# LayerNorm's sums over partitions: an fp32 matmul replaced by two in the linear products' format

## The reference

```python
def _layer_norm(x, g, b):
    mu = mean(x); var = mean(square(x - mu))          # over the channels
    return (x - mu) * rsqrt(var + 1e-5) * g + b

proj = x @ w_in                                       # 1024 -> 1792
attn = window_attention(q, k, v)                      # chunks of 64, window 128, sinks
c    = silu(_layer_norm(dwconv31(u1 * sigmoid(u2)), conv_ln_g, conv_ln_b))   # 512 channels
h    = _layer_norm(ALPHA * x + concat(attn, c) @ w_out, ln1_g, ln1_b)        # 1024
upc  = dwconv3(h @ w_up)                              # 1024 -> 5632
f    = (silu(upc[:D_FF]) * upc[D_FF:]) @ w_down       # 2816 -> 1024
y    = _layer_norm(ALPHA * h + f + sigmoid(h @ w_pg + b_pg) * (p @ w_pe), ln2_g, ln2_b)
```

## Time and profile before

| | |
|---|---|
| median of three runs | 2401.93 us |
| the profiled execution | 2402.03 us, span 2400.1 us |
| TensorE matmuls | 2356.6 us busy, 12733 instructions |
| VectorE | 1388.5 us busy, 2021 instructions |
| ScalarE | 1149.9 us busy |
| GpSimd | 1358.5 us busy, of it 1345.6 in L543 |
| TensorE's mean granted clock | 0.996 of full speed |

### The profile page before, as it was taken

The page is one execution under the profiler, slowest core; times in us unless marked ns, Lnnn a source line. Parts: engine busy times, 40 slices in busy tenths (PEclk is TensorE's granted clock), DMA queues, the critical chain, the costliest instruction groups (busy, mean ns, idle before and its releaser), DMA issues.

```text
span 2400.1 us, 32895 instructions
## 1 busy us (share of the span) xinstructions
PE 2356.6 (98%) x12733; PEld 2189.2 (91%) x12733; DVE 1388.5 (58%) x2021; ACT 1149.9 (48%) x1873; POOL 1358.5 (57%) x1078
## 2 busy tenths in 40 slices
PE   7999999999999999999999999999999999999997
PEld 7988999999988899899998999899889999999996
DVE  5946777634666666426766665257666652663232
ACT  3545654443565443425553535236635353574452
POOL 6654566565644555457545454676555546666663
PEclk9999999999999999999999999999999999999999
DMA  5432334344433333353432332444333324354432
GB/s 190 122 118 88 122 113 126 117 132 145 123 126 111 97 106 107 96 171 108 136 112 89 107 120 82 148 144 146 106 97 106 115 87 153 118 164 139 140 119 86
DMA packets 99978, 289.77 MB, mean 121 GB/s; under 512 B 13424, under 2 KB 37104, under 8 KB 99824
## 3 DMA queue, kind: packets, MB, share of 16 engines
q1 hardware_dynamic: 82560, 261.77, 35.2%
q10 hardware_dynamic: 17264, 25.91, 3.3%
HBM read 278.74 MB, written 8.99 MB: 120 GB/s over the span
## 4 chain that ended last, share of the span: by engine, by line
PE 94%; ACT 2%; DVE 2%; POOL 1%; issue 1%; DMA 0%; DVEq 0%; SPq 0%; ACTq 0%
PE ps L611 30%; PE ps L612 30%; PE ps L613 30%; POOL w_lo L543 1%; PE ps L670 1%; PE ps L702 1%; PE ps L690 1%; PE ps L679 1%; PE ps L717 0%; DVE sq L1329 0%; ACT w_hi L789 0%; DMA x_raw<-in_xT 0%; DMA a_raw<-in_xT 0%; PE ps L751 0%; PE ps L742 0%
## 5 line engine op out<-in xcount | busy, mean ns | idle before, releaser
L543 POOL TENSOR_TENSOR w_lo<-w_raw,w_hi 128x512 fp32r<-128x512 f32 (+2 forms) x1060 | 1345.6, 1296 | 1004.0 <-ACT w_hi L789 998.4
L789 ACT CAST w_hi<-w_raw 128x1024 fp32r<-128x1024 f32 (+2 forms) x529 | 517.0, 982 | 565.0 <-PE ps L613 493.9
L611 PE MATMUL ps<-h_hi,w_hi 128*128 128x450 f32 (+5 forms) x2080 | 743.1, 357 | 7.7 <-POOL w_lo L543 7.7
L612 PE MATMUL ps<-h_lo,w_hi 128*128 128x450 f32 (+5 forms) x2080 | 736.1, 354 | 0.0
L613 PE MATMUL ps<-h_hi,w_lo 128*128 128x450 f32 (+5 forms) x2080 | 735.3, 353 | 0.0
L611 PEld LDWEIGHTS ps<-h_hi,w_hi 128*128 128x128 f32 x2080 | 392.7, 189 | 38.9 <-POOL w_lo L543 9.6
L612 PEld LDWEIGHTS ps<-h_lo,w_hi 128*128 128x128 f32 x2080 | 392.7, 189 | 22.1 <-issue 1.5
L613 PEld LDWEIGHTS ps<-h_hi,w_lo 128*128 128x128 f32 x2080 | 392.3, 189 | 21.1
L611 PE MATMUL ps<-f_hi,w_hi 128*128 128x448 f32 (+2 forms) x1072 | 383.1, 357 | 0.0
L612 PE MATMUL ps<-f_lo,w_hi 128*128 128x448 f32 (+2 forms) x1072 | 377.4, 352 | 0.0
L613 PE MATMUL ps<-f_hi,w_lo 128*128 128x448 f32 (+2 forms) x1072 | 377.4, 352 | 0.0
(11 more groups left out here) (155 smaller groups left out, 1923.1 us busy)
## 6 DMA issues: line engine op xcount, KB each, us to landing
w_raw<-in_panels SPq DMA_DIRECT2D x450, 512.0 KB, 3.5
w_raw<-in_panels SPq DMA_DIRECT2D x40, 384.0 KB, 3.0
xres<-in_xT ACTq DMA_DIRECT2D x24, 224.0 KB, 2.8
out_yT<-res ACTq DMA_DIRECT2D x3, 1792.0 KB, 6.4
w_raw<-in_panels SPq DMA_DIRECT2D x40, 128.0 KB, 2.1
a_raw<-in_xT ACTq DMA_DIRECT2D x4, 896.0 KB, 5.9
x_raw<-in_xT SPq DMA_DIRECT2D x2, 896.0 KB, 5.6
a_raw<-in_xT ACTq DMA_DIRECT2D x2, 768.0 KB, 6.3
```

Of the source, the lines that this page charges most:

```text
L543: ins = pool.tensor_tensor(w_lo[:, n % WS, c], w_raw[:, n % RS, c], w_hi[:, n % WS, c].bitcast(F32), ALU.subtract)
L611: pe.matmul(out, w_hi[:, sl, c], hi, start=first, stop=False)
L612: pe.matmul(out, w_hi[:, sl, c], lo, start=False, stop=False)
L789: act.copy(w_hi[:, n % WS, 0:w], w_raw[:, n % RS, 0:w]).then_inc(w_hi_done, 1)
```

## The change

Twelve of the fifteen LayerNorms are touched, for the mean and the variance each. After the last add, VectorE multiplies the block by 1 (for `cln` by 2) with an output in fp32r, which gives the high part `sum_hi`, and computes the low part `sum_lo` as block times 1 or 2 minus `sum_hi`. TensorE multiplies both by a tile `ones8` of 1/1024 in fp32r and adds them up in PSUM, in place of one f32 matmul. `ones8` is made once by ScalarE from `mean8`. The last add of `tree` and of `running_sum` no longer reports to TensorE but is waited for on VectorE itself.

```diff
+    sum_hi = place("sum_hi", [WM], F32R, offset=sq_base + HB * WM * 4)
+    sum_lo = place("sum_lo", [WM], F32R, offset=sq_base + (HB + 1) * WM * 4)
...
+    ones8 = place("ones8", [P], F32R)
...
                 pe.wait_ge(arrived, SUM_NO[name, t] + 1)
-                pe.matmul(ps[:, b, 0:WIDTH[t]], ones[:], sq[:, 0, 0:WIDTH[t]], start=True, stop=True).then_inc(done, 1)
+                pe.matmul(ps[:, b, 0:WIDTH[t]], ones8[:], sum_hi[:, 0:WIDTH[t]], start=True, stop=False)
+                pe.matmul(ps[:, b, 0:WIDTH[t]], ones8[:], sum_lo[:, 0:WIDTH[t]], start=False, stop=True).then_inc(done, 1)
...
                         act.wait_ge(zero_set, 1)
+                        act.copy(ones8[:], mean8[:])
...
             def tree(src, nb, w, done):
+                blocks = nb
                 while nb > 1:
                     nb //= 2
                     ins = dve.tensor_tensor(sq[:, 0:nb, 0:w], src[:, 0:nb, :], src[:, nb:2 * nb, :], ALU.add)
                     src = sq[:, :, 0:w]
-                    if nb > 1:
-                        own.step(ins)
-                        own.wait()
-                ins.then_inc(done, 1)
+                    own.step(ins)
+                    own.wait()
+                split_sum(w, done, blocks)
+
+            def split_sum(w, done, blocks):
+
+                times, total = float(KB // blocks), sq[:, 0, 0:w]
+                own.step(dve.tensor_scalar(sum_hi[:, 0:w], total, times, None, ALU.mult))
+                own.wait()
+                dve.scalar_tensor_tensor(sum_lo[:, 0:w], total, times, sum_hi[:, 0:w].bitcast(F32), ALU.mult, ALU.subtract
+                                         ).then_inc(done, 1)
...
                 ins = dve.tensor_tensor(total, h_raw[:, 0, c] if m == 1 else total, h_raw[:, m, c], ALU.add)
+                own.step(ins)
                 if m == KB - 1:
-                    ins.then_inc(sum_done, 1)
-                else:
-                    own.step(ins)
+                    own.wait()
+                    split_sum(w, sum_done, KB)
```

## The result

The changed kernel takes 2414.84 us (median of five, 2413.03 to 2415.26) against 2402.0 us: a ratio of 1.005, 95% interval 1.0039 to 1.0061. It is slower by 12.8 us, in the direction to which 0.42 of the chances went, but outside the range of 2399 to 2411. The profiled execution took 2415.03 us, span 2413.1.

What follows compares the result with a forecast made beforehand. TensorE, busy 98% of the span, was taken to bound the kernel. Hold-ups of 12.0 us less a gain of 7.9 made +4.1 us on the profiled 2402.03 (median 2401.93): forecast 2406.0 us, range 2399 to 2411.

Steps and rivals of the forecast that it cites:

- TensorE's gain, 7.9 us: At 24 mean and variance matmuls, fp32r pairs replace f32 products: 0.345 us saved at 448 columns, less at narrower, 7.9 total.
- worth this in full: On TensorE's queue: the whole 7.9 us saved shortens the kernel, since TensorE sets the end.
- The price of the two instructions and the double wait for GpSimd: On VectorE after each sum: about 1.1 us alone, 3.05 us when both instructions wait for GpSimd's halves.
- Rival A: At VectorE's split: tensor_scalar does not contend with GpSimd, hold-ups are half as long, net -2.3, 2399.6 us; chance 0.13.
- Where it reaches TensorE: Ahead of mean matmuls: nine places where TensorE comes too soon after the sum, 0.2 to 3.0 us each, 12.0 together.
- rival C: Behind waits at 1651 and 2058 us: TensorE's granted clock falls, about 1.7 us each, +7.5, 2409.4 us; chance 0.12.
- I add nothing: VectorE work queued behind the split: delays cost 0, covered by several groups of about 4 us through five PSUM banks.
- one of my signs of being wrong: Ahead of L611, TensorE's linear products: a wait that was not there before would show the forecast wrong.
- Range and chances: Whole kernel: 2399 to 2411 us; faster 0.08, no change 0.50, slower 0.42.

Runs made afterwards that it cites:

- TensorE's part alone: Changed kernel without VectorE's split: the last add writes the sum into sum_hi in fp32r, TensorE multiplies it twice, no low part; 2398.39 us, 0.9983 of the original kernel.
- The third run: Changed kernel with the whole sum put in PSUM instead of SBUF, nothing else changed; 2403.86 us, 1.0008 of the original kernel.
- kept-busy: Changed kernel with 16, 18 and 9 overwritten filling matmuls on TensorE in the three longest waits; 2410.25 us, 1.0032 of the original kernel.
- step run: TensorE's part alone plus one f32 product of 8 columns behind each fp32r pair, 24 in all; 2400.49 us, 0.9990 of the original kernel.

## Why the prediction was wrong

- **TensorE's gain, 7.9 us: right in kind, too large.** The spacing at one mean was read rightly (0.36 saved, 0.345 forecast). The term assumed that nothing else on TensorE changes; by the table 7.0 us came in, and 5.65 in the trace of TensorE's part alone. The linear products behind some means now step 4 ns longer, and "worth this in full" leaves out that a TensorE that comes earlier waits longer for `w_lo` at three places (0.6 us) and gains next to nothing where it waits for the sum.
- **The price of the two instructions and the double wait for GpSimd: right.** 3.05 us were forecast behind a contended add; at 1651 us it is 1650.94 to 1653.97, 3.03. The third run confirms the cause: 624 ns each without GpSimd. Rival A is refuted: `tensor_scalar` takes part (0.39 us where nothing holds it up, 1.33 at 1651 us). The Trainium skill's rule ("SBUF — State Buffer", "Who interferes with whom"), by which an instruction with at most one SBUF input and outside the two-port modes doesn't contend, agrees with those 624 ns.
- **Where it reaches TensorE: right.** 12.3 us at nine places, 12.0 at nine forecast, none off by more than 0.3.
- **The clock: the step that failed, with 6.0 of the 8.9 us missing.** I left the fall out of the sum and put it aside as rival C with 0.12, because the kernel before showed it only behind a stop of over 3.4 us, and priced it at two places. It came at four: behind 4.5, 4.2, 2.3 and 2.4 us of idle time (4.3 us at the first three, 1.7 at the last). The two waits of 1.2 and 1.8 us that I had as evidence against it were shorter than any of these. Keeping TensorE busy took 4.6 us away.
- **"I add nothing" for the queue behind the split: failed, 1.7 us.** I argued with the five PSUM banks, which cover evictions. The first `d` group doesn't wait for a bank but for the end of a chain over ScalarE and VectorE that has no room in the last tile; the split at the last variance sits in it. Undoing that one split removed it. A new wait ahead of L611 (now L614) was one of my signs of being wrong, and this is one.
- **Range and chances.** With the falls at the three waits counted in the sum, it would have been 4.1 + 4.3, and 2410 us. The rest, 0.3 of longer waits, 1.7 for `d`, 1.7 at the end and 0.9 of gain, makes up the 13.0 us of the trace. Slower was likelier than I said.

What stays open: ahead of the end of the kernel all twelve traces have the same wait of 2.38 us, but the clock fell behind it in three only (the changed kernel, the kept-busy and the step run) and not in the kernel before or the other eight. So the 1.7 us at the end are in the trace shown, but the change isn't shown to cause them. No run tells what decides it; it may be when the waits before it came. The same goes for the length of a fall, at 505 us and behind the waits for the sum (3.4 or 6.8 us by kernel). These make single totals differ by 1.2 to 1.7 us, and conclusions finer than that rest on the traces' distances, one execution each.

## What to carry to other kernels

An engine at 58% isn't idle where it counts: list, for each hand-over to the engine that bounds the kernel, how long after the hand-over the latter comes, and compare the new work with that, including what it waits for on a memory port. When a change makes TensorE stand still for as long as the 2.3 to 4.5 us seen here, put a fall of its clock into the sum, about 1.4 us each; it is a cost of the wait and not an unlikely extra. And a gain that is the same at 24 places should be taken only at those that have the room: 18 of them, with the sum in PSUM away from GpSimd, made a slowdown of 12.8 us into a gain of 3.8.

## What the runs showed of the hardware that I had not expected

- Linear products of 448 columns in fp32r have two steps, 202.7 and 206.7 ns, each held over hundreds of instructions. An f32 product, even one of 8 columns, ahead of a stretch gave the shorter one in a stretch where two fp32r products gave the longer.
- In all twelve traces the granted clock fell (windows of 0.51 to 0.57) behind every idle time of the load queue of 2.3 to 4.9 us later than 60 us, but for the one of 2.38 us ahead of the end, where it fell in three traces of twelve. It fell behind none of the shorter ones, up to 2.02 us. The low stretch lasted 3.4 us or twice that.
- A `tensor_scalar` from PSUM to SBUF took 624 ns for 448 columns, as long as the two-input form; from SBUF to SBUF it took about 0.25 us once GpSimd let go (at 1651 us GpSimd's half ends at 1650.41 + 1.65 = 1652.06, the `tensor_scalar` at 1650.97 + 1.33 = 1652.30), 0.39 to 0.40 where GpSimd held nothing up (seven places), 0.94 in the mean with the waiting.
